# Windowed attention by pairs of heads and blocks of 128 queries, with the softmax's division folded into the product that turns each block

## The reference, cut to what matters

```python
s = jnp.einsum('bhrnqd,bhrnkd->bhrnqk', qb * dh ** -0.5, kw) + bias[None, :, None, None]
s = jnp.where(valid, s, NEG_INF)
m = jnp.max(s, axis=-1, keepdims=True)
e = jnp.exp(s - m)
denom = jnp.sum(e, axis=-1, keepdims=True)
o = jnp.einsum('bhrnqk,bhrnkd->bhrnqd', e, vw) / denom
lse = (m + jnp.log(denom))[..., 0]
...
w = jax.nn.softmax(jnp.stack(lses), axis=0)
o = jnp.sum(w[..., None] * jnp.stack(outs), axis=0)
```

## Time and profile before

| | us |
|---|---|
| median of three runs | 2958.32 |
| lowest, highest | 2954.82, 2960.21 |
| profiled execution, its own time | 2962.57 |
| span of the profiled execution | 2960.8 |
| attention, first scores to last product of values | 221.7 to 285.8 |

### The profile page before, as it was taken

The page is one execution under the profiler, slowest core; times in us unless marked ns, Lnnn a source line. Parts: engine busy times, 40 slices in busy tenths (PEclk is TensorE's granted clock), DMA queues, the critical chain, the costliest instruction groups (busy, mean ns, idle before and its releaser), DMA issues.

```text
span 2960.8 us, 37075 instructions
## 1 busy us (share of the span) xinstructions
PE 2822.4 (95%) x15702; PEld 2244.9 (76%) x15702; DVE 1445.8 (49%) x1856; ACT 1136.4 (38%) x1393; POOL 227.8 (8%) x203
## 2 busy tenths in 40 slices
PE   6998889999999999999999999989999999999998
PEld 4875767888877777677778888877786777788886
DVE  6483547443466545345574444555443254643322
ACT  4375244222244442535443222344425354432222
POOL 1010401000021100011010000010100100100001
PEclk9998999999999999999999999999999999999999
DMA  8430004443331123122243433321231211322221
GB/s 317 154 150 27 3 16 164 156 149 132 118 128 68 54 106 133 69 105 86 72 156 142 155 141 135 111 73 70 81 123 43 88 57 46 119 92 100 90 99 54
DMA packets 46944, 309.68 MB, mean 105 GB/s; under 512 B 5531, under 2 KB 6427, under 8 KB 13500
## 3 DMA queue, kind: packets, MB, share of 16 engines
q1 hardware_dynamic: 44684, 297.33, 27.6%
q0 software_dynamic: 2096, 10.00, 0.9%
HBM read 302.58 MB, written 4.72 MB: 104 GB/s over the span
## 4 chain that ended last, share of the span: by engine, by line
PE 84%; ACT 7%; DVE 5%; issue 3%; DMA 1%; SPq 0%; ACTq 0%; DVEq 0%; POOL 0%
PE bank L2191 64%; PE bank L2125 5%; PE bank L2503 2%; PE bank L2313 2%; PE bank L2523 2%; PE bank L2176 2%; ACT WH L915 1%; DMA raw<-in_wstream_dram 1%; PE bank L2649 1%; DVE WL L1473 1%; PE bank L2514 1%; DVE raw L1513 1%; ACT L1000 1%; PE bank L2539 1%; PE bank L2275 0%
## 5 line engine op out<-in xcount | busy, mean ns | idle before, releaser
L2191 PE MATMUL bank<-HH,WH 128*128 128x512 f32 x2256 | 911.1, 404 | 29.8 <-DVE HL L1586 13.8
L2191 PE MATMUL bank<-HH,WL 128*128 128x512 f32 x2256 | 885.1, 392 | 0.0
L2191 PE MATMUL bank<-HL,WH 128*128 128x512 f32 x2256 | 884.9, 392 | 0.0
L1473 DVE TENSOR_TENSOR WL<-raw,WH 128x2048 fp32r<-128x2048 f32 (+2 forms) x263 | 489.9, 1864 | 654.1 <-ACT WH L915 653.2
L2191 PEld LDWEIGHTS bank<-HH,WH 128*128 128x128 f32 x2256 | 425.7, 189 | 138.7 <-issue 28.2
L915 ACT ACTIVATE WH<-raw 128x2048 fp32r<-128x2048 f32 (+3 forms) x223 | 395.5, 1774 | 333.0 <-PE bank L2191 320.2
L2191 PEld LDWEIGHTS bank<-HL,WH 128*128 128x128 f32 x2256 | 425.7, 189 | 95.0 <-issue 7.9
L2191 PEld LDWEIGHTS bank<-HH,WL 128*128 128x128 f32 x2256 | 425.2, 188 | 94.0
L2191 PE MATMUL bank<-AH,WH 128*128 128x512 f32 x492 | 193.9, 394 | 0.0
L2191 PE MATMUL bank<-AH,WL 128*128 128x512 f32 x492 | 192.9, 392 | 0.0
L2191 PE MATMUL bank<-AL,WH 128*128 128x512 f32 x492 | 190.9, 388 | 0.0
(11 more groups left out here) (378 smaller groups left out, 3531.9 us busy)
## 6 DMA issues: line engine op xcount, KB each, us to landing
raw<-in_wstream_dram SPq DMA_DIRECT2D x256, 1024.0 KB, 4.8
raw<-in_wstream_dram SPq DMA_DIRECT2D x24, 512.0 KB, 3.5
raw<-in_wstream_dram SPq DMA_DIRECT2D x12, 768.0 KB, 4.3
bgam<-in_consts_dram POOLq DMA_DIRECT2D x2, 1792.0 KB, 7.1
bias_dram<-bias_row POOLq DMA_DIRECT2D x8, 320.0 KB, 6.6
xT<-in_x_dram SPq DMA_DIRECT2D x2, 1024.0 KB, 8.4
toep<-bias_dram POOLq DMA_DIRECT2D x8, 256.0 KB, 3.2
out_dram<-ost SPq DMA_DIRECT2D x4, 512.0 KB, 2.7
```

The lines of the kernel that those rows point to most:

```text
L1473: TT(WL[:, wi % 2, now], raw[:, j.load % RAW, now], WH[:, wi % 2, now].bitcast(F32), ALU.subtract).then_inc(s["w_split"], 2 if half is Non ...
L2191: last = MM(o[m][0:cw, :], a, b, start=j.first and u == 0 and q == 0, stop=j.last and u == j.units - 1 and q == 2)
```

## The change

The attention now has twenty steps t. A step is one block of queries i = t % 4 of one pair of heads p = t // 4, with both heads e = 0, 1 side by side.

- PE, step t: turns block t-2, computes the scores of block t for both heads (rows 0 to 63 and rows 64 to 127, one product after the other, into two banks), then multiplies values by block t-3. Each turn is now a full product of the piece of `Sx` with `inverse_sums`, a 128x128 tile that has the inverse sums on its diagonal, so it turns and scales at once. The product of values is cut into pieces of 128 columns, the two heads in turn.
- DVE, step t: bias, maximum and `anmax` of block t, then the inverse sums of block t-1 and its two diagonal tiles (`ident` times the inverse sum). `Sx` itself is no longer scaled.
- ACT, step t: copies block t-2, exponentials of block t.
- POOL: a fourth slot for the bias tiles, in a part of `HH` that is free once the projections are done.

`Sx` and `PT` now hold a pair of heads in one buffer, and the scores, maxima, sums and diagonal tiles have two buffers by the block's parity. The diff, without the lines that only change counts of semaphores:

```diff
@@ -129,8 +129,8 @@
                   11: [("length", 3), ("unit", 2)], 12: [("conv", 6), ("unit", 3)]}.get(i, [])
-    for h in range(10):
-        steps.append(("attn", h))
+    for t in range(20):
+        steps.append(("attn", t))
...
@@ -434,6 +434,8 @@

+        toeps = [toep[:, x, :] for x in range(3)] + [spare("toep_late", 1, 4)[:, :]]
+        inverse_sums = spare("inverse_sums", 1, 5)[:, :].rearrange("p (x e q) -> p x e q", x=2, e=2)
...
@@ -644,6 +646,10 @@

+        def segment(t):
+
+            return slice(SEG[t % 4], SEG[t % 4] + P * (t % 4 + 1))
+
...
@@ -754,12 +760,14 @@
             def toeplitz(h):
-                if h >= 3:
-                    pool.wait_ge(s["a_biased"], 4 * (h - 2))
+                if h == 3:
+                    pool.wait_ge(s["gemm_done"], gemm_before(ATTENTION))
+                elif h > 3:
+                    pool.wait_ge(s["a_biased"], 8 * (h // 2 - 1))
                 pool.wait_ge(s["bias_stored"], 16 * 8)
                 skew = bass.AP(bias_dram.tensor, bias_dram.offset + h * P * TOEP + P - 1,
                                [[TOEP - 1, P], [1, S]])
-                pool.dma_start(toep[:, h % 3, :], skew).then_inc(s[f"toep{h % 3}"], 16)
+                pool.dma_start(toeps[h % 4], skew).then_inc(s[f"toep{h % 4}"], 16)
...
@@ -824,10 +832,11 @@
                     pool.dma_start(aw[0:32, :, :], walpha_in[st[2] - 1]).then_inc(s["c_in"], 16)
-                if st[0] == "attn" and st[1] < 8:
-                    h = st[1]
-                    if h >= 1 and h + 2 < 8:
-                        toeplitz(h + 2)
+                if st == ("attn", 0):
+                    toeplitz(3)
+                if st[0] == "attn" and st[1] in (4, 8):
+                    for h in range(st[1], st[1] + 2) if st[1] == 4 else range(6, 8):
+                        toeplitz(h)
...
@@ -1130,30 +1139,29 @@

-            def attention(h):
-
-                g = h - 2
+            def attention(t):
+
+                g = t - 2
                 if g == 0:
-
                     act.wait_ge(s["dn_scaled"], 4)
-                if g >= 0:
+                if 0 <= g < 16:
                     act.wait_ge(s["a_turned"], g + 1)
-                    if g >= 2:
-                        act.wait_ge(s["a_out"], g - 1)
-                    for b, a, e in ((0, 0, 512), (1, 512, 1024), (2, 1024, 1280)):
-                        A(PT[:, g % 2, a:e], bank[b][:, 0:e - a], ACT.Copy).then_inc(s["a_turn_copied"], 1)
-                if h < 8:
-                    act.wait_ge(s["a_nmax"], h + 1)
-                    for i in range(NT):
-                        seg = slice(SEG[i], SEG[i] + P * (i + 1))
-                        A(Sx[:, h % 2, seg], Sx[:, h % 2, seg], ACT.Exp, bias=anmax[:, h % 2, i:i + 1],
-                          accum_out=asum[:, h % 2, i:i + 1]).then_inc(s["a_exp"], 1)
-                if g >= 0 and g % 2:
-                    act.wait_ge(s["a_out"], g + 1)
-                    if g == 1:
+                    if g >= 4:
+                        act.wait_ge(s["a_out"], g - 3)
+                    for e in range(2):
+                        A(PT[:, e, segment(g)], bank[e][:, 0:P * (g % 4 + 1)], ACT.Copy
+                          ).then_inc(s["a_turn_copied"], 1)
+                if t < 16:
+                    act.wait_ge(s["a_nmax"], t + 1)
+                    for e in range(2):
+                        A(Sx[:, e, segment(t)], Sx[:, e, segment(t)], ACT.Exp, bias=anmax[:, t % 2, e:e + 1],
+                          accum_out=asum[:, t % 2, e:e + 1]).then_inc(s["a_exp"], 1)
+                if t >= 6 and t % 4 == 2:
+                    pair = (t - 6) // 4
+                    act.wait_ge(s["a_out"], 4 * pair + 4)
+                    if pair == 0:
                         act.wait_ge(s["gemm_done"], gemm_before(ATTENTION))
-                    A(HH[:, g // 2, :], bank[3 if g // 2 % 2 else 7][:, :], ACT.Copy
-                      ).then_inc(s["a_high"], 1)
+                    A(HH[:, pair, :], bank[2 + pair % 2][:, :], ACT.Copy).then_inc(s["a_high"], 1)
...
@@ -1680,35 +1688,39 @@

-            def attention(h):
-
-                g = h - 1
-                if 0 <= g < 8:
-                    dve.wait_ge(s["a_exp"], 4 * g + 4)
-                    dve.reciprocal(arsum[:, g % 2, :], asum[:, g % 2, :]).then_inc(s["a_rsum"], 1)
+            def attention(t):
+
+                if t < 16:
+                    p, i = divmod(t, 4)
+                    dve.wait_ge(s["a_scores"], t + 1)
+                    if t >= 4:
+                        dve.wait_ge(s["a_turned"], t - 3)
+                    for e in range(2):
+                        h = 2 * p + e
+                        if i == 0:
+                            dve.wait_ge(toep_in[h % 4], 16 * (h // 4 + 1))
+                        dve.tensor_tensor_reduce(Sx[:, e, segment(t)], bank[4 + 2 * (t % 2) + e][:, 0:P * (i + 1)],
+                                                 toeps[h % 4][:, 384 - P * i:512], 1.0, -3.0e38,
+                                                 ALU.add, ALU.max, amax[:, t % 2, e:e + 1]
+                                                 ).then_inc(s["a_biased"], 1)
+                    dve.wait_ge(s["a_biased"], 2 * t + 2)
+                    TS(anmax[:, t % 2, 0:2], amax[:, t % 2, 0:2], -1.0, None, ALU.mult).then_inc(s["a_nmax"], 1)
+                g = t - 1
+                if 0 <= g < 16:
+                    dve.wait_ge(s["a_exp"], 2 * g + 2)
+                    dve.reciprocal(arsum[:, g % 2, 0:2], asum[:, g % 2, 0:2]).then_inc(s["a_rsum"], 1)
                     dve.wait_ge(s["a_rsum"], g + 1)
-                    for i in range(NT):
-                        seg = slice(SEG[i], SEG[i] + P * (i + 1))
-                        TS(Sx[:, g % 2, seg], Sx[:, g % 2, seg], arsum[:, g % 2, i:i + 1], None, ALU.mult
+                    if g >= 2:
+                        dve.wait_ge(s["a_turned"], g - 1)
+                    elif g == 0:
+                        dve.wait_ge(s["gemm_done"], gemm_before(ATTENTION))
+                    for e in range(2):
+                        TS(inverse_sums[:, g % 2, e, :], ident[:, :], arsum[:, g % 2, e:e + 1], None, ALU.mult
                            ).then_inc(s["a_norm"], 1)
-                if h < 8:
-                    dve.wait_ge(s["a_scores"], h + 1)
-                    dve.wait_ge(toep_in[h % 3], 16 * (h // 3 + 1))
-                    if h >= 2:
-                        dve.wait_ge(s["a_turned"], h - 1)
-                    for i in range(NT):
-                        b, c0 = SBANK[i]
-                        seg = slice(SEG[i], SEG[i] + P * (i + 1))
-                        dve.tensor_tensor_reduce(Sx[:, h % 2, seg], bank[b][:, c0:c0 + P * (i + 1)],
-                                                 toep[:, h % 3, 384 - P * i:512], 1.0, -3.0e38,
-                                                 ALU.add, ALU.max, amax[:, h % 2, i:i + 1]
-                                                 ).then_inc(s["a_biased"], 1)
-                    dve.wait_ge(s["a_biased"], 4 * h + 4)
-                    TS(anmax[:, h % 2, :], amax[:, h % 2, :], -1.0, None, ALU.mult).then_inc(s["a_nmax"], 1)
-                if h >= 2 and h % 2:
-                    pair = (h - 2) // 2
+                if t >= 7 and t % 4 == 3:
+                    pair = (t - 7) // 4
                     dve.wait_ge(s["a_high"], pair + 1)
-                    TT(HL[:, pair, :], bank[3 if pair % 2 else 7][:, :], HH[:, pair, :].bitcast(F32), ALU.subtract
+                    TT(HL[:, pair, :], bank[2 + pair % 2][:, :], HH[:, pair, :].bitcast(F32), ALU.subtract
...
@@ -2246,45 +2258,45 @@

-            def attention(h):
-
-                g = h - 2
-                if g >= 0:
-                    pe.wait_ge(s["a_norm"], 4 * g + 4)
+            def attention(t):
+
+                g = t - 2
+                if 0 <= g < 16:
+                    i = g % 4
+                    pe.wait_ge(s["a_norm"], 2 * g + 2)
                     if g:
-                        pe.wait_ge(s["a_turn_copied"], 3 * g)
+                        pe.wait_ge(s["a_turn_copied"], 2 * g)
                     else:
-
                         pe.wait_ge(s["act_evac"], JOBS[LAST_IN].act)
-                    for jb in range(NT):
-                        for i in range(jb, NT):
-                            b, c0 = TBANK[jb]
-                            src = Sx[:, g % 2, SEG[i] + P * jb:SEG[i] + P * jb + P]
-                            last = pe.transpose(bank[b][:, c0 + P * (i - jb):c0 + P * (i - jb) + P], src,
-                                                ident[:, :])
+                    for jb in range(i + 1):
+                        for e in range(2):
+                            at = SEG[i] + P * jb
+                            last = MM(bank[e][:, P * jb:P * jb + P], Sx[:, e, at:at + P],
+                                      inverse_sums[:, g % 2, e, :], start=True, stop=True)
                     last.then_inc(s["a_turned"], 1)
-                if h < 8:
```

(53 more changed lines are left out.)

## The result

| us | before | changed |
|---|---|---|
| median of 6 runs | 2957.93 | 2967.66 |
| lowest, highest | 2954.82, 2960.21 | 2964.44, 2971.71 |
| profiled execution | 2962.57 | 2964.44 |
| its attention, first scores to first product of the recurrence | 221.7 to 285.8 | 221.9 to 292.4 |

The ratio is 1.0033, 95% interval 1.0022 to 1.0043: slower by 9.7 us. The two profiled executions alone would say 1.9: that of before lies above all its six timed runs, that of the changed kernel is its fastest. In them the attention's end moved by 6.6; what follows the attention took 2675.0 us before and 2670.2 after.

What follows compares the result with a forecast made beforehand. TensorE bounds the steady attention now; the new order makes a ring, per pair 7.4 + 4.05 + 2.46 + 1.7 = 15.6 against 12.34. With 1.4 at full clock and 4 for the clock, +5.4: median 2963.7, range 2952 to 2976.

Steps and rivals of the forecast that it cites:

- The ring: Attention: scores, bias, tiles of the block before, products, next scores follow one another; 15.6 us per four blocks against 12.34.
- DVE's part: DVE's work in the attention: bias and maximum 3.8, anmax, reciprocal and tiles 3.6, so 7.4 us per pair of heads.
- The price of a product: TensorE's turning: 0.203 us a product against 0.124 a transpose, twenty costing 4.05 instead of 2.48 per pair.
- Full-clock end: End of the attention at full clock: 287.2, which is 1.4 us later than now.
- first scores to first products: Start of the attention: after two exponentials 0.8, reciprocal and tiles 0.8, the first products start at 225.8.
- thirteen turns: Steady attention, from bias of block 2 at 227.3 to block 15 at 278.1: 13 x 3.9 = 50.8 us.
- the end: Last steps of the attention, from bias and maximum of block 15 through its values, each in turn: 9.1 us.
- The clock: Attention's start: the clock falls at 226 as before, costing 4 us; no more in later turns.
- The first rival: Clock stays at 1.2 GHz or falls again from gaps in each turn: median 2990, in half the turns 2975; chance 0.17.
- Values: TensorE's product of values, 40 records per pair: between 2.7 and 4.05 us, middle taken; before 4.60.
- The faster rival: Attention: the ring doesn't bind, TensorE's own work does; -8 us, 2950; chance 0.13.
- The rules that were cited: Skill's fourfold-faster transposes would make twenty products 9.9 a pair, some 20 us lost; changing tiling mode drains TensorE, trace 0.10.

Runs made afterwards that it cites:

- cut at DVE: Changed kernel with DVE making the tiles of block t-1 before it waits for the scores of block t; median 2951.99, ratio 0.9979.
- transposes: Changed kernel with transposes in place of the products with the diagonal tiles, division by the sums left out; median 2954.49, ratio 0.9989.
- dummies in all gaps: Changed kernel plus TensorE products nobody reads, three before the first tiles and one in each of steps 2 to 14; median 2959.31, ratio 1.0004.
- scores_first: Changed kernel with TensorE taking the scores of block t ahead of the products of block t-2; median 2944.98, ratio 0.9956.
- two dummies: Kernel before plus two 512-column TensorE products nobody reads, after the scores of head 0; median 2953.09, ratio 0.9992.

## Why the prediction came out as it did

The way was forecast, slower because of the ring, and the range held; 5.4 was forecast and 9.7 measured. By its steps:

- **The ring.** Shown: cut at TensorE it gives 11.4 per four blocks, cut at DVE 12.7, and with a cheaper part in it (transposes) 13.2, against 15.76, where 15.6 was forecast. The sum was right in part by luck: products with the ends of their trains cost 0.65 + 1.09 + 1.54 + 1.98 = 5.3 where 4.45 was taken (4.85 with the first weight load), and DVE's part is 6.8 where 7.4 was taken (the reciprocal at 280.40 follows `anmax` at 280.33 after 0.07, not 0.20, since it doesn't wait for it).
- **The price of a product** was mis-read, 0.203. In the changed kernel trains of 4, 8, 12 and 16 records take 0.65, 1.09, 1.54 and 1.98 us to the start of the next group: 0.112 for each further record, so 0.223 a product, and about 0.20 for the two ends of a train. The single starts in the trace stand 0.112 apart as well. They do so too in the train that I had divided, but the product behind it starts 0.03 us after the last of its eight records (918.71 to 919.52), so that record was counted at almost nothing. Transposes stand 0.109 apart, with 0.15 for the ends, and my 0.124 held these ends. This makes 20 x (0.223 - 0.109) = 2.3 and 0.2 for the ends of four trains, the 2.5 of the transposes. What sets 0.112 is open: the records of the dummies, four times as wide, stand 0.43 apart, so the width alone gives 0.107.
- **Full-clock end.** 287.2 forecast, 288.7 with dummies in all gaps, in an execution whose attention starts 0.9 us later. Its parts hold as well: first scores to first products 4.16 us (4.1 forecast), thirteen turns from 228.31 to 279.68, 51.4 (50.8), the end 9.03 (9.1).
- **The clock** is the term that was mis-sized: 4 taken, 7 to 9 measured, and 4.4 and 9.7 in the two profiles (70.6 and 75.9 less 66.2). That the first profile nearly met the sum, 292.4 for 291.2, is luck: some 2.0 of its 4.4 were lost at the start, where all 4 were expected, and 2.4 in the steady part, where none was. The step that failed is "Later turns keep TensorE busy some 60 to 70%, and in the recurrence two windows ... keep the full clock, so I take no more". The clock fell in such turns, in another place in each execution. The profile before had given a sign, its own second fall at 276.8, which the prediction did not weigh. The first rival, given 0.17, named this; its figure for half of the turns, 2975, is too high.
- **Values**: 2.8 by the starts in scores_first, near the lower bound of 2.7, and off the path in the changed kernel.
- **The faster rival** was right in what it priced: without the ring, TensorE's own 11.4 per four blocks is the period and the kernel takes 2945, which it put at 2950. What it lacked is the order, which the rows of the order showed.
- **The rules that were cited.** The Trainium skill says that transpose mode is four times faster for FP32 (TensorE: Matmul & The Clock Gate, Terms). By that a product would cost 0.50, an estimate from the rule and the 0.124 of a transpose; the trace has 0.223 against 0.109, twice. That different tiles can work in parallel (the Trainium skill, TensorEngine Tiling (Array Packing), Key Properties) is borne out for the two column halves, with 0.055 us a record against 0.109.

Left open: which of the long waits the clock falls behind, since two executions of one program differ.

## What to carry to other kernels

When two engines pass each other's results, write down for each the order inside one step and follow one item around: if engine A's next item waits for B's last, and B's for A's, the period is the sum of both parts, however little each is busy. Moving one independent group of instructions ahead of a wait cut it here, 23 us for no work at all. A new order with short gaps has a second price in the clock that one profile does not size; take two or more. And read the price of a product from trains of different length, not from one short train divided by its records: the difference of two trains is free of what their ends cost.

## What the runs showed of the hardware

- Records of a float32 product of 128 columns with a full set of new weights stand 0.112 us apart and transposes of the same piece 0.109; a product is two records, a transpose one. The two ends of a train add about 0.20 and 0.15 us. Records of 512 columns stand 0.43 apart.
- Pairs of products on the two halves of the columns (128 rows, 64 columns each): 0.055 us a record while both run, 0.109 while one does. Issued one half after the other, the last records of the first still overlapped the first of the second.
- TensorE at 1.2 GHz can cost less than the doubled times say. In the kernel before it ran so from 225.6 to 242.6 and from 276.8 to 280.2 of the attention. With two dummies 3.4 of these 20.5 us were left and the attention ended 4.4 us earlier, since waits took the place of slow work; the gain in the whole time, 2.7 us, is not told from none.
- In the changed kernel, with TensorE busy some 70% of the steady part, the clock fell there in every profile without dummies in the gaps, each time within 1.2 us of the end of a wait of 1.8 to 1.9 us. In the one profile with dummies in all gaps, where only the wait that ends at 281.8 was longer than 1.3 us, it stayed full.
